# A streaming encoder step on one core: attention loads moved ahead, rope scores over 128 rows, another order of query tiles and fill

## The chip, the core and the metric

The kernel runs on one core of one Trainium2 chip. A core has five engines that run side by side, each with its own queue of instructions in a fixed order: TensorE (PE: matrix products, with weight loads as PEld), VectorE (DVE), ScalarE (ACT), GpSimd (POOL) and SyncE (SP, which here only issues transfers). They wait for each other by semaphores. The time is the device time of one execution in microseconds (us); the kernel before took 3075.96 us in the median of three runs (3072.53 to 3084.09).

## The reference

One inference step of a two-layer encoder over 1024 prompt rows and 32 sample rows (1056 together, width 1024). Layer 0 has a gated linear attention, layer 1 a latent attention (MLA) with 8 heads; each layer ends with a gated MLP (width 2816) with a causal convolution. The change touches the MLA:

```python
s = (jnp.einsum('bqhd,bkhd->bhqk', qn, k_nope) + jnp.einsum('bqhd,bkd->bhqk', qp, k_pe)) * scale
mask = k_chunk[None, :] <= (qpos // CHUNK)[:, None]          # CHUNK = 64
p = jax.nn.softmax(jnp.where(mask, s, -jnp.inf), axis=-1)
o = jnp.einsum('bhqk,bkhd->bqhd', p.astype(v.dtype), v)      # then o @ w_out, added to x
```

A query has a part of 128 numbers per head (`qn`, "nope") and a rotated part of 64 (`qp`, "rope"); `k_pe`, the rope key, is shared by the heads. Prompt queries see the prompt keys of their own 64-row chunk and of those before; sample queries see 512 cached keys and their own 32. All is float32.

## The kernel before

**Precision.** Most products are made of three passes in the fast float32 form (fp32r): each operand is split into a high part (a copy by ScalarE into fp32r) and a low part (raw minus high, by GpSimd). `mm3` (lines 275 to 277) then issues high x high, high x low, low x high. The splits of the attention are `akh`/`akl` (keys), `aqh`/`aql` (queries), `aph`/`apl` (rope queries), `kph`/`kpl` (rope keys), `moh`/`mol` (output weights) and `oh`/`ol` (attention output).

**Stages.** Layer 0, then the latent projection (`act_mla`, `dve_mla`, `pe_mla`: among others the rope keys, with cached ones in columns 1024 to 1535), then for four pairs of heads the projections of keys, values and queries (`PREP`, a list of units; results go to DRAM by `sp_prep`), then attention, then layer 1's MLP.

**Attention.** 72 steps, 9 per head: `STEPS` (line 1335) takes tiles t = 0 to 7 (128 queries against 128(t+1) keys) and then t = 8 (32 sample queries against 544 keys), ascending in each head. In step s TensorE does, in this order (`pe_att`): the scores of step s in pieces of up to 512 keys (`score`), the transposes of the probabilities of step s-1 (`turn`, line 1423, and 1425 for the 32 queries), a fill tile, the weighing of the values of step s-2 (`weigh`, line 1439), and another fill tile. Between scores and transposes the step goes through VectorE (mask 1561, maximum 1563, negation 1565), ScalarE (exponential 1518) and VectorE again (reciprocal 1569, scaling of `aP` 1571). ScalarE also copies the transposes out (1511) and makes `oh` (1528); VectorE makes `ol` (1578).

A piece of scores is an `mm3` over the 128 nope rows and an `mm3` over 64 rope rows. The rope queries of two heads lie in one buffer, in rows 0 to 63 and 64 to 127; the rope keys stand in both halves.

**Fill.** The output projection of a pair (24 tiles, each six matmuls of 352 columns into bank 7, then an addition on VectorE, line 443) is spread over the steps of the next pair by `FILL`: two tiles a step in steps 2 to 13 of 18. The last pair's 24 tiles come after all steps.

**Loads.** SyncE issues all transfers in one queue. `sp_att` loads keys (`load_k`), queries, rope queries (once a pair) and values of heads 0 and 1 behind everything that `sp_prep` stores, later heads two ahead of use. The output weights have one buffer: their load waits for the fill of the pair before, and the loads of heads 4 and 6 stand behind it. ScalarE's splits of head h+1 stand in its queue at tiles 3 (keys), 4 (queries) and, per pair, 6 (rope queries) of head h, the output weights at tile 7 of odd heads.

## Time and profile before

| | |
|---|---|
| median of 3 runs | 3075.96 us (3072.53 to 3084.09) |
| the profiled execution | 3070.57 us |
| its span, first to last instruction | 3068.6 us |
| mean granted TensorE clock | 0.959 |
| PE busy | 2852.2 us, 93% |
| PEld busy | 2680.6 us, 87% |
| DVE busy | 1202.8 us, 39% |
| ACT busy | 897.5 us, 29% |
| POOL busy | 690.2 us, 22% |
| chain that ended last | PE 39%, issue 36%, POOL 13%, DVE 8%, ACT 3%, DMA 1% |

A busy TensorE is not one at its peak: a matmul's record covers its way through the array, and records overlap. The distance from the start of one matmul to the start of the next is what it costs in a stream. "Clock" is the share of 2.4 GHz that was granted; 0.50 is 1.2 GHz. The chain is followed back from the last instruction through what released each one; "issue" is time in which nothing that the profile shows was waited for.

### The profile page before, as it was taken

Reading aid. Unit: us, or ns where it says so; the run is one execution under the profiler, and the core shown is the slowest. Engines: PE = TensorE matmul, PEld = TensorE weight load, DVE = VectorE, ACT = ScalarE, POOL = GpSimd, SP = SyncE. Lnnn points to the kernel's source line nnn. Section 1 sums busy time; section 2 is a strip of 40 time slices with the busy share of each in tenths; the row PEclk is TensorE's granted clock in tenths of the full one; section 3 lists DMA queues with packets and bytes.
Section 4 is the critical chain, followed back from the end, with each engine's and each line's share of the span. In section 5 each row is a group of like instructions: output and inputs, shape, how many; then the busy total and the mean of one; then the engine's idle time right before and its main releaser. Section 6 shows DMA issues by size and latency. Waiting matters only on the chain.

```text
span 3068.6 us, 42405 instructions
## 1 busy us (share of the span) xinstructions
PE 2852.2 (93%) x17373; PEld 2680.6 (87%) x17373; DVE 1202.8 (39%) x2169; ACT 897.5 (29%) x1530; POOL 690.2 (22%) x233
## 2 busy tenths in 40 slices
PE   6899999989999999999799969897989999999998
PEld 4888898979999999999788857676779999999998
DVE  5534443444333233324623334444463233233333
ACT  4332323243111111112346644233332211111111
POOL 2111111123322222231321112112032322322230
PEclk8899999999999999999999979898989999999999
DMA  2011111011111111111113231102001111111112
GB/s 93 16 32 30 31 43 31 30 31 42 42 43 47 51 42 42 56 42 42 60 53 119 106 140 64 49 29 77 28 14 56 42 42 55 43 42 42 56 42 72
DMA packets 155743, 154.74 MB, mean 50 GB/s; under 512 B 14897, under 2 KB 137407, under 8 KB 155439
## 3 DMA queue, kind: packets, MB, share of 16 engines
q1 hardware_dynamic: 153231, 150.03, 15.1%
q8 instruction: 150, 2.46, 0.3%
q10 hardware_dynamic: 2336, 2.03, 0.2%
q14 instruction: 26, 0.21, 0.0%
HBM read 125.89 MB, written 26.15 MB: 50 GB/s over the span
## 4 chain that ended last, share of the span: by engine, by line
PE 39%; issue 36%; POOL 13%; DVE 8%; ACT 3%; DMA 1%; SPq 0%; POOLq 0%; ACTq 0%; DVEq 0%
POOL wlo L256 9%; PE ps L275 9%; PE ps L276 8%; PE ps L277 8%; POOL falo L624 3%; PE ps L1439 2%; PE ps L1232 1%; PE ps L1423 1%; DVE ge L919 1%; PE ps L692 1%; DVE sq_rest L336 1%; DMA apraw<-s_p 1%; DVE xT L443 1%; PE ps L679 1%; DVE aP L1571 1%
## 5 line engine op out<-in xcount | busy, mean ns | idle before, releaser
L275 PE MATMUL ps<-hh,whi 128*128 128x352 f32 (+1 forms) x2688 | 879.9, 327 | 40.7 <-POOL hl L399 12.6
L276 PE MATMUL ps<-hl,whi 128*128 128x352 f32 (+1 forms) x2688 | 867.7, 323 | 0.0
L277 PE MATMUL ps<-hh,wlo 128*128 128x352 f32 (+1 forms) x2688 | 867.0, 323 | 0.0
L256 POOL TENSOR_TENSOR wlo<-wraw,whi 128x2048 fp32r<-128x2048 f32 (+1 forms) x87 | 393.8, 4527 | 970.3 <-ACT whi L249 923.0
L275 PEld LDWEIGHTS ps<-hh,whi 128*128 128x128 f32 (+1 forms) x2688 | 506.4, 188 | 51.7 <-issue 47.6
L276 PEld LDWEIGHTS ps<-hl,whi 128*128 128x128 f32 (+1 forms) x2688 | 507.4, 189 | 3.5 <-issue 1.1
L277 PEld LDWEIGHTS ps<-hh,wlo 128*128 128x128 f32 (+1 forms) x2688 | 505.8, 188 | 2.4 <-issue 0.2
L443 DVE TENSOR_TENSOR xT<-xT,ps 128x352 f32<-128x352 f32 x720 | 374.0, 521 | 340.2 <-PE ps L277 339.1
L275 PE MATMUL ps<-fahi,whi 128*128 128x352 f32 x1056 | 346.2, 328 | 16.2 <-POOL falo L624 10.4
L276 PE MATMUL ps<-falo,whi 128*128 128x352 f32 x1056 | 342.8, 325 | 0.0
L277 PE MATMUL ps<-fahi,wlo 128*128 128x352 f32 x1056 | 342.7, 325 | 0.0
L249 ACT ACTIVATE whi<-wraw 128x2048 fp32r<-128x2048 f32 (+1 forms) x83 | 157.2, 1894 | 632.4 <-DMA wraw<-w_ffn_in 453.9
L583 DVE TENSOR_SCALAR fc<-fg,par 128x1058 f32<-128x1058 f32 x44 | 39.1, 889 | 517.1 <-ACT fg L561 517.1
L624 POOL TENSOR_TENSOR falo<-fa,fahi 128x1056 fp32r<-128x1056 f32 x44 | 108.2, 2459 | 582.6 <-ACT fahi L566 582.6
L275 PEld LDWEIGHTS ps<-fahi,whi 128*128 128x128 f32 x1056 | 200.4, 190 | 23.7 <-DVE xT L443 12.2
L276 PEld LDWEIGHTS ps<-falo,whi 128*128 128x128 f32 x1056 | 200.3, 190 | 0.5 <-issue 0.5
L277 PEld LDWEIGHTS ps<-fahi,wlo 128*128 128x128 f32 x1056 | 200.2, 190 | 0.0
L599 DVE TENSOR_TENSOR fa<-fc,ps 128x352 f32<-128x352 f32 (+2 forms) x176 | 63.7, 425 | 249.3 <-PE ps L277 247.0
L566 ACT ACTIVATE fahi<-fa 128x1056 fp32r<-128x1056 f32 x44 | 47.8, 1086 | 265.1 <-DVE fa L599 265.1
L564 ACT ACTIVATE fc<-fc 128x1058 f32<-128x1058 f32 x44 | 48.0, 1090 | 184.7 <-DVE fc L593 184.7
L1511 ACT ACTIVATE aPT<-ps 128x384 f32<-128x384 f32 (+3 forms) x112 | 47.0, 449 | 179.1 <-PE ps L1423 154.8
L1439 PE MATMUL ps<-aPT,av 128*128 128x128 f32 (+2 forms) x656 | 95.4, 295 | 0.8 <-DVE ol L1578 0.8
(269 smaller groups left out, 4206.8 us busy)
## 6 DMA issues: line engine op xcount, KB each, us to landing
wraw<-w_ffn_in SPq DMA_DIRECT2D x88, 512.0 KB, 5.0
wraw<-w_ffn_out SPq DMA_DIRECT2D x44, 512.0 KB, 4.0
wraw<-w_gla_in SPq DMA_DIRECT2D x24, 512.0 KB, 4.6
s_k<-kw SPq DMA_DIRECT2D x8, 784.0 KB, 3.3
akraw<-s_k SPq DMA_DIRECT2D x8, 784.0 KB, 5.5
s_v<-vst SPq DMA_DIRECT2D x8, 768.0 KB, 3.9
av<-s_v SPq DMA_DIRECT2D x8, 768.0 KB, 5.8
s_q<-qw SPq DMA_DIRECT2D x8, 528.0 KB, 2.7
```

The source lines that it names most:

```text
L249: act.activation(hi[:, 0:cols], raw[:, 0:cols], ACT.Copy).then_inc(S("w_hi"), 1)
L256: pool.tensor_tensor(lo[:, 0:cols], raw[:, 0:cols], hi[:, 0:cols].bitcast(F32), ALU.subtract).then_inc(S("w_lo"), 1)
L275: nc.tensor.matmul(out, w[0], x[0], start=start, stop=False)
L276: nc.tensor.matmul(out, w[0], x[1], start=False, stop=False)
L277: return nc.tensor.matmul(out, w[1], x[0], start=False, stop=stop)
L443: dve.tensor_tensor(xT[:, m, tc(j)], xT[:, m, tc(j)], ps[:, banks[i % len(banks)], 0:TC], ALU.add)\
L564: act.activation(fc[:, par_, 0:CW], fc[:, par_, 0:CW], ACT.Gelu).then_inc(S("gelu"), 1)
L566: act.activation(fahi[:, gpar, par_, :], fa32[:, gpar, par_, :], ACT.Copy).then_inc(S("a_hi"), 1)
L599: last = dve.tensor_tensor(fa32[:, gpar, par_, t0:t0 + n], fc[:, par_, col:col + n], ps[:, B_BANKS[j], a:a + n], ALU.mult)
L624: pool.tensor_tensor(falo[:, gpar, par_, :], fa32[:, gpar, par_, :], fahi[:, gpar, par_, :].bitcast(F32), ALU.subtract).then_inc(S("a_lo"), 1)
L1439: last = pe.matmul(ps[:, 6, 0:m], av[h % 2][0:n, kk0 // P, :], aPT[s % 2][0:n, i, 0:m], start=(i == 0), stop=(i == len(tiles) - 1))
L1511: act.activation(buf[:, i0:i0 + nt, 0:m], src[:, :, 0:m], ACT.Copy).then_inc(S("probsT"), 1)
```

## The change

- **Rope scores.** `khl` takes the place of `kpl`: high rope keys in rows 0 to 63, low ones in rows 64 to 127. `kph` keeps the high keys in rows 0 to 63, and its rows 64 to 127 are made zero by subtracting them from themselves. The rope queries of a head are loaded twice, into both halves of a buffer of its own. One matmul of `aph` with `khl` then gives high x high + high x low, one of `apl` with `kph` low x high: two matmuls of 128 rows for three of 64. ScalarE and GpSimd split rope queries for each head instead of each pair. The latent projection has three ScalarE copies more into `khl` and one VectorE subtraction (64 x 1568) more.
- **Loads.** Head 0 is loaded in `sp_prep` of the last pair behind the value stores, head 1 behind its rope store; ScalarE's splits of head 0 stand behind the last query unit instead of behind all units. The output weights have two buffers: the load for pair p waits only for the fill of the pair two before.
- **Order.** Even heads take tiles 7, 6, 5, 4, 3, 8, 2, 1, 0, odd heads 0, 1, 2, 8, 3, 4, 5, 6, 7. The splits keep their place in the head (its steps 3, 4 and now 5; the output weights step 7 of the odd head).
- **Fill.** One tile in steps 2 to 4 and 14 to 16, two in steps 5 to 13.

```diff
-        K_AT, KL_AT = (W, H), (W + 4096, H + NKEY)
+        K_AT, KL_AT = (W + 2048 - NKEY, H), (W + 4096, H + NKEY)
...
-        moh = at("moh", [P, 2 * D], W + 2048, F32R)
...
+        MO_AT, MOL_AT = (R + 18272 - 176 - 2352, W + 2048), (W + 2048 - NKEY - 2 * D, R + 6 * NKEY)
+        moh = [at(f"moh{i}", [P, 2 * D], MO_AT[i], F32R) for i in range(2)]
...
+        def load_p(sp, h):
+            for a in range(2):
+                sp.dma_start(apraw[h % 2][a * ROPE:(a + 1) * ROPE, :],
+                             A["s_p"][h // 2][h % 2 * ROPE:(h % 2 + 1) * ROPE, :]).then_inc(S(f"head_loaded{h % 2}"), 16)
...
+            if p == MP - 1:
+                sp.wait_ge(S("k_left0"), 16)
+                load_k(sp, 0)
+                wait_unit(sp, (p, "v", 0, 6))
+                wait_unit(sp, (p, "k", 1, 3))
+                sp.wait_ge(S("q_left"), 16)
+                load_q(sp, 0)
+                sp.wait_ge(S("p_left"), 16)
+                load_p(sp, 0)
+                sp.wait_ge(S("v_left"), 64)
+                load_v(sp, 0)
             if p:
                 k_out(1)
             sp.wait_ge(S("rope_sum"), NCH * (p + 1))
             sp.dma_start(A["s_p"][p], pw[:, :]).then_inc(S("p_left"), 16)
+            if p == MP - 1:
+                wait_unit(sp, (p, "q", 1, 2))
+                sp.wait_ge(S("k_left1"), 16)
+                load_k(sp, 1)
+                load_q(sp, 1)
+                load_v(sp, 1)
+                sp.wait_ge(S("k_left0"), 16 * MP)
+                load_p(sp, 1)
             q_out(1)
...
-        STEPS = [(h, t) for h in range(MH) for t in range(9)]
+        UP = [0, 1, 2, 8, 3, 4, 5, 6, 7]
+        STEPS = [(h, t) for h in range(MH) for t in (UP if h % 2 else UP[::-1])]
...
-        FILL = [0, 0] + [2] * 12 + [0] * 4
+        FILL = [0, 0, 1, 1, 1, 2, 2, 2, 2, 2, 2, 2, 2, 2, 1, 1, 1, 0]
...
-                    last = mm3(out, (aph[pr][half, qs_], apl[pr][half, qs_]), (kph[half, keys], kpl[half, keys]),
-                               False, True)
+                    pe.matmul(out, aph[sl][:, qs_], khl[:, keys], start=False, stop=False)
+                    last = pe.matmul(out, apl[sl][:, qs_], kph[:, keys], start=False, stop=True)
...
-                    pe.wait_ge(S("o_lo"), NS - 9 + (3, 6, 9)[i // KD])
+                    pe.wait_ge(S("o_lo"), NS - 9 + (3, 7, 9)[i // KD])
...
-                if h % 2:
-                    sp.wait_ge(S("down_mm"), fill_before(h // 2))
-                    load_mo(h // 2)
+                if h % 2 == 0:
+                    sp.wait_ge(S("down_mm"), fill_before(h // 2 - 1))
+                    load_mo(sp, h // 2)
...
+            act.activation(khl[0:ROPE, 0:SEQ], kpe[0:ROPE, 0:SEQ], ACT.Copy)
...
+                if PREP[u] == (MP - 1, "q", 1, 2):
+                    head_split(act, 0)
+                    q_split(act, 0)
+                    p_split(act, 0)
...
+            dve.tensor_tensor(kph[low, :], kph[low, :].bitcast(F32), kph[low, :].bitcast(F32), ALU.subtract)\
+               .then_inc(S("latent_lo"), 1)
```

SyncE's queue at the end of the projections, before (`s_p`, `s_q`, `s_k`, `s_v` are the DRAM buffers, `kw`, `vst`, `pw` and `qw` what is stored there, the names in `raw` and `av` what attention reads):

```order
149 L1330 DMA s_p<-pw 128x1056
150 L1315 DMA s_q<-qw 128x1056
151 L1594 DMA akraw_142<-s_k 128x1568
152 L1597 DMA aqraw_148<-s_q 128x1056
153 L1600 DMA apraw_154<-s_p 128x1056
154 L1604 DMA av_156<-s_v 128x1536
155 L1606 DMA av_156<-s_v 32x128
156 L1594 DMA akraw_143<-s_k 128x1568
```

and now:

```order
148 L1298 DMA akraw_142<-s_k 128x1568
149 L1301 DMA aqraw_148<-s_q 128x1056
150 L1305 DMA apraw_154<-s_p 64x1056 x2
151 L1310 DMA av_156<-s_v 128x1536
152 L1312 DMA av_156<-s_v 32x128
153 L1335 DMA s_k<-kw_119 128x1568
154 L1365 DMA s_p<-pw 128x1056
155 L1298 DMA akraw_143<-s_k 128x1568
156 L1301 DMA aqraw_149<-s_q 128x1056
157 L1310 DMA av_157<-s_v 128x1536
158 L1312 DMA av_157<-s_v 32x128
159 L1305 DMA apraw_155<-s_p 64x1056 x2
```

The four loads of head 0 moved ahead of the last key and rope stores; those of head 1 stand between the rope store and the last query store, with the rope queries last.

TensorE's queue within head 0, the 640-key tile and the start of the next, before (`akh`, `akl`, `aqh`, `aql` nope keys and queries, `kph`, `kpl`, `aph`, `apl` rope ones, `aP` probabilities, `aPT` their transposes, `av` values):

```order
4432 L275 MATMUL ps<-akh_138,aqh_144 128x128
4433 L276 MATMUL ps<-akl_140,aqh_144 128x128
4434 L277 MATMUL ps<-akh_138,aql_146 128x128
4435 L275 MATMUL ps<-kph,aph_150 128x128
4436 L276 MATMUL ps<-kpl,aph_150 128x128
4437 L277 MATMUL ps<-kph,apl_152 128x128
4438 L1423 MATMUL ps<-ident,aP_159 128x128 x4
4439 L1439 MATMUL ps<-aPT_160,av_156 128x128 x3
4440 L275 MATMUL ps<-akh_138,aqh_144 128x512
```

and now, in its second step (the 896-key tile, behind the 1024-key one):

```order
4407 L276 MATMUL ps<-akh_138,aqh_144 128x512
4408 L277 MATMUL ps<-akl_140,aqh_144 128x512
4409 L278 MATMUL ps<-akh_138,aql_146 128x512
4410 L1450 MATMUL ps<-khl,aph_150 128x512
4411 L1451 MATMUL ps<-kph,apl_152 128x512
4412 L276 MATMUL ps<-akh_138,aqh_144 128x384
4413 L277 MATMUL ps<-akl_140,aqh_144 128x384
4414 L278 MATMUL ps<-akh_138,aql_146 128x384
4415 L1450 MATMUL ps<-khl,aph_150 128x384
4416 L1451 MATMUL ps<-kph,apl_152 128x384
4417 L1466 MATMUL ps<-ident,aP_158 128x128 x8
```

A piece of scores has five matmuls instead of six, all of them over 128 rows, and the eight transposes of the largest tile now come behind the second step's scores.

## Rows read from the trace of the kernel before

**Rows 1.** Stretches; columns in the first line.

```profile
core 0: us, PE busy (x) PEld busy (x) DVE busy (x) ACT busy (x) POOL busy (x), PEclk, DMA share, GB/s
1796.22:1819.81 23.59, 0.00 (x0) 0.03 (x1) 3.32 (x6) 5.09 (x5) 8.23 (x3) 0.60 0.77 296
1819.81:1889.99 70.18, 67.91 (x388) 50.48 (x389) 36.37 (x101) 35.77 (x84) 16.19 (x6) 0.92 0.13 44
1889.99:2005.73 115.74, 99.15 (x571) 81.11 (x570) 50.31 (x130) 38.12 (x91) 19.09 (x7) 0.88 0.14 52
...
2118.95:2229.45 110.50, 103.46 (x608) 85.25 (x606) 52.15 (x134) 35.91 (x93) 13.42 (x4) 0.93 0.11 36
1893.00:1900.00 7.00, 6.70 (x30) 6.35 (x31) 1.74 (x8) 1.13 (x6) 0.00 (x0) 0.51 0.00 1
1987.00:1995.00 8.00, 8.00 (x35) 6.29 (x36) 3.67 (x10) 2.61 (x7) 2.19 (x1) 0.69 0.00 0
```

**Rows 2.** Waits from 1796 to 2230: total, times, longest, in us.

```profile
ACT akh L1480 <- DMA apraw<-s_p: 46.0, 3, 17.6
...
PE ps L1423 <- DVE aP L1571: 27.8, 4, 13.4
...
PE ps L275 <- POOL apl L1588: 23.6, 1, 23.6
...
PE ps L1425 <- DVE aP L1571: 9.9, 4, 3.0
```

**Rows 3.** Timeline of TensorE, scores of a 1024-key tile: start, length.

```profile
1931.39 0.39 PE L275 MATMUL ps<-akh,aqh 128*128 128x512 f32 x1
1931.62 0.39 PE L276 MATMUL ps<-akl,aqh 128*128 128x512 f32 x1
...
1933.63 0.40 PE L277 MATMUL ps<-akh,aql 128*128 128x512 f32 x1
1933.96 0.50 PE L275 MATMUL ps<-kph,aph 64*128 64x512 f32 x1
1934.30 0.39 PE L276 MATMUL ps<-kpl,aph 64*128 64x512 f32 x1
1934.53 0.38 PE L277 MATMUL ps<-kph,apl 64*128 64x512 f32 x1
1934.85 0.98 PE L1423 MATMUL ps<-ident,aP 128*128 128x128 f32 x7
```

**Rows 4.** Timeline of SyncE: transfers issued.

```profile
1779.64 0.50 SPq L1325 DMA_DIRECT2D s_v<-vst  x1
...
1800.24 0.46 SPq L1594 DMA_DIRECT2D akraw<-s_k  x1
...
1971.82 0.43 SPq L1594 DMA_DIRECT2D akraw<-s_k  x1
```

**Rows 5.** GpSimd's subtractions by form: busy us, mean ns of one.

```profile
L1588 POOL TENSOR_TENSOR akl<-akraw,akh 128x1568 fp32r<-128x1568 f32 x8 | 28.2, 3522 | 289.5 <-ACT akh L1480 289.5
...
L1588 POOL TENSOR_TENSOR mol<-moraw,moh 128x2048 fp32r<-128x2048 f32 x4 | 18.0, 4512 | 79.0 <-ACT moh L1543 79.0
...
L1588 POOL TENSOR_TENSOR apl<-apraw,aph 128x1056 fp32r<-128x1056 f32 x4 | 9.8, 2442 | 23.1 <-ACT aph L1488 23.1
```

**Rows 6.** Timeline of VectorE: mask and scaling of one step, and a held scaling.

```profile
1849.26 0.11 DVE L1561 MEMSET ps<- 64x64 f32 x1 [1.61 <-PE ps L277]
...
1852.29 0.75 DVE L1571 TENSOR_SCALAR aP<-aP,rl 128x1024 f32<-128x1024 f32 x1
...
1890.24 3.00 DVE L1571 TENSOR_SCALAR aP<-aP,rl 32x544 f32<-32x544 f32 x1
```

**Rows 7.** Timeline in the latent projection: ScalarE's copy, and TensorE's wait.

```profile
1532.71 0.60 ACT L1789 ACTIVATE kph<-ps 128x512 fp32r<-128x512 f32 x1
...
1535.76 0.63 PE L275 MATMUL ps<-hh,whi 128*128 128x352 f32 x1 [3.18 <-ACT cqr L1794]
```

More of the change, by code:

```diff
@@ L1294, in dve_unit, with load_k, load_q, load_v @@
                                          ALU.mult, ALU.mult).then_inc(S("normed"), 1)
+        def load_k(sp, h):
+            sp.dma_start(akraw[h % 2][:, :], A["s_k"][h]).then_inc(S(f"head_loaded{h % 2}"), 16)
+        def load_q(sp, h):
+            sp.dma_start(aqraw[h % 2][:, :], A["s_q"][h]).then_inc(S(f"head_loaded{h % 2}"), 16)
+        def load_p(sp, h):
+            for a in range(2):
+                sp.dma_start(apraw[h % 2][a * ROPE:(a + 1) * ROPE, :],
+                             A["s_p"][h // 2][h % 2 * ROPE:(h % 2 + 1) * ROPE, :]).then_inc(S(f"head_loaded{h % 2}"), 16)
+        def load_v(sp, h):
+            n = (KT - 1) * P
+            sp.dma_start(av[h % 2][:, 0:KT - 1, :].rearrange("p t v -> p (t v)"), A["s_v"][h][:, 0:n])\
+              .then_inc(S(f"av_loaded{h % 2}"), 16)
+            sp.dma_start(av[h % 2][0:DEC, KT - 1, :], A["s_v"][h][0:DEC, n:n + P])\
+              .then_inc(S(f"av_loaded{h % 2}"), 16)
+        def load_mo(sp, p):
+            v = moraw[p % 2][:, :].rearrange("p (k n) -> p k n", k=2)
+            for a in range(2):
+                sp.dma_start(v[:, a, :], w_mout[:, 2 * p + a, :]).then_inc(S("mo_loaded"), 16)
         def sp_prep(sp, p):
@@ L1365, in fill_before, with mo_view @@
             return 24 * (B_MLA + p)
-        def mo_view():
-            return [w[:, :].rearrange("p (k n) -> p k n", k=2) for w in (moh, mol)]
+        def mo_view(p):
+            return [w[p % 2][:, :].rearrange("p (k n) -> p k n", k=2) for w in (moh, mol)]
         def pe_pair_tile(pe, p, i, bank):
@@ L1374, in pe_pair_tile @@
             for k in range(2):
-                last = mm3(ps[:, bank, 0:TC], [v[:, k, m * P:(m + 1) * P] for v in mo_view()],
+                last = mm3(ps[:, bank, 0:TC], [v[:, k, m * P:(m + 1) * P] for v in mo_view(p)],
                            (oh[o][:, k, tc(j)], ol[o][:, k, tc(j)]), k == 0, k == 1)
@@ L1380, in build @@
         LAST_BANKS = (7, 4, 5, 6)
-        SPLITS = [("k", 0), ("q", 0), ("p", 0), ("k", 1), ("q", 1)]
-        for h in range(2, MH):
-            SPLITS += [("k", h), ("q", h)] + ([("p", h // 2), ("mo", h // 2 - 1)] if h % 2 == 0 else [])
+        SPLITS = []
+        for h in range(MH):
+            SPLITS += [("k", h), ("q", h), ("p", h)] + ([("mo", h // 2 - 1)] if h and h % 2 == 0 else [])
         SPLITS += [("mo", MP - 1)]
@@ L1525, in act_att @@
                     act.wait_ge(S("att_mm"), s - 1)
-                    if t == 0 and h % 2 == 0 and p >= 2:
+                    if (s - 2) % 18 == 0 and p >= 2:
                         act.wait_ge(S("down_mm"), fill_before(p - 1))
@@ L1561, in dve_att @@
                         dve.memset(flat[0:64, c0 + nk - 64:c0 + nk], MASKED).then_inc(S("masked"), 1)
-                        dve.wait_ge(S("masked"), h * 8 + t + 1)
+                        dve.wait_ge(S("masked"), sum(t_ < NG for _, t_ in STEPS[:s + 1]))
                     dve.tensor_reduce(mx[0:m, two], flat[0:m, c0:c0 + nk], AX.X, ALU.max).then_inc(S("max"), 1)
@@ L1788, in act_mla @@
             act.wait_ge(S("cache_mm"), 3)
[L1789 removed]
+            act.activation(kph[:, SEQ:SEQ + PAST], ps[:, A_BANKS[0], 0:PAST], ACT.Copy)
+            act.activation(khl[0:ROPE, SEQ:SEQ + PAST], ps[0:ROPE, A_BANKS[0], 0:PAST], ACT.Copy)\
+               .then_inc(S("latent_hi"), 1)
             act.wait_ge(S("kpe_sb"), 1)
```

120 lines of the change are left out of this document (43 added, 77 removed).

## Prediction

> **What bounds the kernel now.** I read the page first: TensorE is busy 93% of the span, and the chain that ended last is a third TensorE work, a third "issue". So the place to look is where TensorE is not doing useful columns. The change touches only the attention stage and a few instructions of the latent projection ahead of it, so I cut that stage out with stretches of time [rows 1]: attention with its fill runs from 1819.81 to 2229.45, 409.6 us, as one pair of heads without fill (70.2 us) and three pairs with 24 fill tiles each (115.7, 113.2 and 110.5; the middle one is what the other stretches leave of the 409.6). Before it TensorE stands still for 23.6 us, at a mean clock of 0.60.
>
> The waits of that stage [rows 2] name three kinds of idle time: 23.6 us once, for the low half of the rope queries (GpSimd); 27.8 us in four waits, the longest 13.4, for the softmax's scaled rows; 9.9 us in four waits for the same thing ahead of the 32-row tile. ScalarE's 46.0 us for a DMA say why the first two exist: the key load of heads 4 and 6 leaves late [rows 4] and the cast of it stands in ScalarE's queue ahead of the exponentials.
>
> Then the matmuls one by one [rows 3]: with 128 rows behind 128 rows a 512-column matmul follows in 0.23 us (1931.39 to 1931.62). Between the nope part (128 rows) and the rope part (64 rows) it takes 0.33 (1933.63 to 1933.96) and the one after it 0.34; leaving the rope part takes 0.32 again (1934.53 to 1934.85). So each change of row count costs 0.21 us more than the columns do, and a 64-row matmul costs what a 128-row one does.
>
> **The change, part by part, against the profiled execution (3070.6 us; the runs' median is 3076.0, 5.4 above it).**
>
> *Rope scores in 128 rows.* (a) One of six matmuls of each score piece goes, 112 in all. Per head the pieces are seven of 512 columns, two of 384, two of 256, two of 128 and one of 32. At 0.23 for 512 and, in proportion with a floor near 0.12 (estimate; the weight load), 0.17, 0.12, 0.12, 0.03 for the others: 1.6 + 0.34 + 0.24 + 0.24 + 0.03 = 2.5 us a head. (b) The changes of row count go: 14 times into the rope part and 5 times out of it to a second piece, 0.21 each, and 9 times out of it to the transposes, of which I take only the half seen on the rope side (0.32 instead of 0.23 at 1934.53 to 1934.85), less 0.5 for the 32-row tile: 2.9 + 1.05 + 0.9 - 0.5 = 4.4 us a head. Together 6.9 us, times 8 = **-55 us** of TensorE work (bounds: 20, only the matmuls; 62, both halves of each change).
>
> The Trainium skill ("TensorEngine Tiling (Array Packing)", Key Properties) says that a change of tiling mode drains the engine. The rows above agree for 128 to 64 rows. By the rule read strictly the 32-query tile is a change too and would keep its cost, some 0.2 us twice a head, 3 us in all; the sum above is without it.
>
> *Loads in order.* The loads of head 0 stood behind the last query store, at 1800.24. Now they follow the value stores of the last pair, which left by 1779.64 + 0.50 [rows 4]; about 2.7 MB at 385 GB/s (296 at a DMA share of 0.77 in the gap, [rows 1]) is there by 1790. ScalarE casts them behind the last query copy (about 1793.5 by my estimate, some 2.7 us before TensorE ends the projection at 1796.2), GpSimd's three subtractions follow from 1795.0: 3.5 + 2.5 + 2.4 [rows 5] = 8.4, so scores start at 1803.5. The gap shrinks from 23.6 to 7.3: **-16.3**. What is late next is GpSimd, no longer a DMA. Nothing hides that chain.
>
> With two buffers for the output weights, the loads of heads 4 and 6 no longer wait for the fill of the pair before. The two stalls (13.4 and 12.3, in the 27.8 of [rows 2]) go, and with each the slow clock behind it: 8 us at 0.69 [rows 1] are 2.5 us each. **-30**. Head 4's loads leave at step 27 and its cast stands at step 30, some 13 us later, for a 7 us transfer: covered.
>
> *What the same edits add.* Head 1's loads now stand behind rope_sum, which DVE finishes only behind GpSimd's subtractions (its SBUF-to-SBUF operations hold while GpSimd runs: a scaling of 544 columns took 3.00 us at 1890.24 beside the 4.5 us subtraction, where one of 1024 takes 0.75 [rows 5, 6]), near 1804.5. Four loads, 3.2 MB with the store ahead, land near 1814; the cast of head 1's keys stands in ScalarE's queue behind the first exponential, about 1811: 3 us of waiting, with the exponentials of step 1 behind it and TensorE behind these.
>
> *Order of the tiles.* In head 0, the large tile comes first: its chain (mask, maximum, exponential, scaling) is 1849.26 to 1853.04, 3.8 us [rows 6], and 4.1 with the hops, and only 2.4 us of score matmuls stand beside it. VectorE is at both ends of that chain, so no step is shorter than its chain. With TensorE's work cut (a 1024-key step: ten score matmuls 2.4, and by estimate from the tiles' number transposes 0.8 and weighing 1.25, together 4.5 instead of 5.6) the steps of small tiles without fill become chain-bound: 128 to 512 keys have a chain of about 1.9 to 2.7 (estimate from the same chain with fewer columns) against 0.9 to 1.8 of TensorE work. In pair 0 that is 5 us over six steps, 3 at the start, 3 for the load above, about 4 for the half clock under large tiles instead of small ones, 2 for GpSimd's subtractions under shorter steps: **+17**. Pair 0 keeps its 70 us or so, its 14 us of saved TensorE work gone.
>
> In pairs 1 to 3 every step has TensorE work above its chain (smallest margin: the 1024-key steps, 4.4 against 4.1), because the fill is spread over steps 2 to 16: the fill of 24 tiles itself stays the same. The first of these pairs shows 99.2 us of busy TensorE in 115.7 [rows 1]; the clock's deficit is 0.12 of 115.7 = 13.9 us, about 8 of it inside the 16.6 us in which TensorE stood, so some 5.6 us of the busy time are slow clock and 93.6 are work. Less 2 x 6.9 that is 80 us a pair.
>
> *GpSimd.* Four rope subtractions more (2.4 each). Their casts stand where steps take 4 to 5 us with fill, and VectorE's scaling falls outside. The output weight's subtraction (4.5 us) now stands one step earlier, under the scaling of the last 1024-key tile: 2.0 us late instead of the 2.5 before the 32-row tile, with 2.4 us of scores beside it instead of 0.85. Before it cost 2.3 us and 7 us at half clock, 3.4 lost [rows 1]. I take 2 us less over the four, and 2 less for waits behind the first fill tile: **-2 to -4**, taken as -2.
>
> The Trainium skill ("SBUF — State Buffer", Who interferes with whom) says that the shared port is an exclusive lock for a tensor_scalar in a fast mode and for a tensor_tensor with both inputs in SBUF, and that the later one blocks to the end. The 3.00 us row agrees. By the rule at its worst, all 85 us of GpSimd's passes lie over a VectorE scaling, each up to its own length; that is rival 2 below.
>
> *Projection.* ScalarE has 0.6 us more (the copy of the cached rope keys, [rows 7]) ahead of the logarithm for which TensorE waits 3.2 us: **+0.5**. The other copies and VectorE's subtraction of the rows with themselves stand beside matmuls of 11 us and cost nothing; without that cover they would cost 3.
>
> Sum: -55 - 16.3 - 30 - 2 + 17 + 0.5 = **-86**, and 2 us less at the end, where the large tile's wait of about 4 us is followed by half of the transposes and weighings that stood there: -88. Profile 2983, median 2988.
>
> **The rivals.**
> 1. *Only the matmuls go* (10%). What I read as the cost of changing the row count comes from new weights and stays. For: the extra is at both ends of a group. Against: fill to nope has none of it. Then -88 + 35 = -53: 3023.
> 2. *Short steps run into the chain, the loads and GpSimd's lock* (15%). Pair 0 costs 85 instead of 71, and each of pairs 1 to 3 loses 4 us more under the casts, with the clock falling behind each gap, as it did for 7 us behind one of 2.3. -88 + 26: 3014. For: the margins of the 1024-key steps are 0.3 us. Against: the three pairs with fill had only the waits named in [rows 2].
> 3. *Slower: the clock* (3%). TensorE now has idle time in nearly every step of pair 0 and less work in the others, and the granted clock stays at its lower level (1.2 GHz) instead of 2.4 through much of the stage. The stage has some 315 us of work: from 90 us of work at half clock on, the gain is used up; with half the stage, 157 us, it is slower by 70: 3146. For: it was 0.51 in the 7 us behind a short wait [rows 1]. Against: pair 0 of before, short steps and a cold start in it, still had 0.92 on the mean [rows 1].
> 4. *More than I take* (7%): both halves of every change of row count go (7 us more) and the first steps hide the load: 2972.
>
> **How the numbers follow.** 65% for the forecast, 2972 to 3003 its own range. Rivals 1 and 2 reach to 3023, so the range is 2966 to 3023. A measurement of this kernel tells 0.5% (15 us) from no change. Faster by more than that: all but rival 3, and what I can't name: 0.94; within 0.02; slower 0.04.
>
> **What would show it.** In the profile after: score matmuls of 512 columns following each other in 0.23 with no 0.33 among them; TensorE's gap ahead of attention near 7 us, ended by GpSimd; no wait over 5 us at heads 4 and 6; pair 0 near 70 us and pairs 1 to 3 near 82 to 85 each. I am wrong if pair 0 grows beyond 80, if the pairs with fill stay above 92, or if a step with fill waits for VectorE.

## The result, and the profile after

The changed kernel took 2972.40 us in the median of four runs (2969.68 to 2973.62), the kernel before 3074.99 in four runs beside it (3072.53 to 3084.09): a ratio of 0.966, 95% interval 0.9639 to 0.9681. The forecast was 2988 with a range of 2966 to 3023. The direction and the range held; the gain is 15 us larger than forecast (102.6 for 88).

The profiled execution after took 2972.77 us, its span is 2970.7 at a mean clock of 0.969. First the same stretches as in [rows 1]: the gap ahead of attention, then the four pairs of heads, the last up to the first tile of its own output projection (columns: stretch, us, busy us of each engine with its instructions, granted clock, DMA share, GB/s).

```profile
1803.43:1811.16 7.73, 0.00 (x1) 0.03 (x1) 7.52 (x4) 3.06 (x5) 7.59 (x3) 0.78 0.00 0
1811.16:1879.55 68.39, 56.28 (x359) 48.94 (x359) 37.14 (x104) 35.49 (x85) 18.58 (x7) 0.90 0.38 128
1879.55:1961.83 82.28, 79.46 (x544) 72.70 (x542) 49.45 (x130) 39.23 (x92) 22.22 (x8) 1.00 0.25 79
1961.83:2043.44 81.61, 79.49 (x543) 72.66 (x542) 48.77 (x130) 39.21 (x92) 21.56 (x8) 1.00 0.24 80
2043.44:2135.12 91.68, 85.83 (x582) 78.69 (x580) 51.32 (x134) 38.50 (x94) 15.71 (x5) 0.98 0.13 40
```

Attention is 323.96 us long where it was 409.64 (-85.7), and the gap ahead of it 7.73 where it was 23.59 (-15.9); the two make 101.5. (The two profiled executions differ by 97.8: in the one after, the projections ended 7.2 us later, and what lies behind attention was 3.6 shorter.) Of the 85.7, pair 0 gives 1.8, the next two pairs 33.5 and 31.6, the last 18.8. The two pairs that lost most are those in which a stall of 13.4 and 12.3 us stood. The clock is at 1.00 through both now; it was 0.88 and 0.91.

What TensorE waited for in attention after (view of the waits: total, times, longest), in answer to [rows 2]:

```profile
PE ps L1466 <- DVE aP L1611: 18.3, 14, 7.1
PE ps L276 <- POOL apl L1628: 7.7, 1, 7.7
PE ps L276 <- DVE xT L444: 3.4, 12, 0.4
...
PE ps L1468 <- DVE aP L1611: 0.4, 1, 0.4
```

The wait for scaled rows has gone from 27.8 us in four to 18.3 in fourteen: the two long stalls went, and one of 7.1 us and thirteen of 0.3 to 2.9 came. The 9.9 us ahead of the 32-row tile are 0.4.

Scores of a 1024-key tile after, on TensorE's timeline, in answer to [rows 3]:

```profile
1958.42 0.39 PE L1451 MATMUL ps<-kph,apl 128*128 128x512 f32 x1
1958.64 0.40 PE L276 MATMUL ps<-akh,aqh 128*128 128x512 f32 x1
1958.88 0.40 PE L277 MATMUL ps<-akl,aqh 128*128 128x512 f32 x1
1959.12 0.40 PE L278 MATMUL ps<-akh,aql 128*128 128x512 f32 x1
1959.35 0.39 PE L1450 MATMUL ps<-khl,aph 128*128 128x512 f32 x1
1959.58 0.39 PE L1451 MATMUL ps<-kph,apl 128*128 128x512 f32 x1
1959.81 0.38 PE L1466 MATMUL ps<-ident,aP 128*128 128x128 f32 x2
```

Every start is 0.22 to 0.24 behind the one before, into and out of the rope part too; the 0.33 are gone.

The new wait of 7.1 us is the one thing in this profile that the forecast had much smaller. Its story, on four engines (start, length; in brackets the idle time ahead and what ended it):

```profile
1800.62 1.51 ACT L1521 ACTIVATE akh<-akraw 128x1568 fp32r<-128x1568 f32 x1
1800.95 0.52 DVE L1285 TENSOR_TENSOR pw<-pw,cos 128x352 f32<-128x352 f32 x1
1802.21 3.51 POOL L1628 TENSOR_TENSOR akl<-akraw,akh 128x1568 fp32r<-128x1568 f32 x1 [47.65 <-ACT akh L1521]
1802.64 3.46 DVE L1285 TENSOR_TENSOR pw<-pw,cos 128x352 f32<-128x352 f32 x1
1811.50 0.53 DVE L1288 TENSOR_TENSOR pw<-pw,arp 128x352 f32<-128x352 f32 x1
1812.06 0.32 SPq L1365 DMA_DIRECT2D s_p<-pw  x1
1823.63 1.51 ACT L1521 ACTIVATE akh<-akraw 128x1568 fp32r<-128x1568 f32 x1 [5.36 <-DMA apraw<-s_p]
1829.25 1.76 PE L1466 MATMUL ps<-ident,aP 128*128 128x128 f32 x7 [7.11 <-DVE aP L1611]
```

GpSimd starts on head 0; the rotation of the rope queries on VectorE, whose multiplications take 0.52 us, takes 3.46 beside it; SyncE, which waits for the last sum, issues the rope store at 1812.06 and head 1's loads behind it; ScalarE waits 5.36 us for them with an exponential behind, and TensorE 7.11.

### The profile page after: what moved, and what is told of

It reads as the page before. It is cut to its first block, busy times and chain, and to the rows that moved or that the text cites. A ratio compares the mean times of both kernels' runs of the same rounds, so it can differ in the third digit from the quotient of the medians.

```text
span 2970.7 us, 42205 instructions
## 1 busy us (share of the span) xinstructions
PE 2787.6 (94%) x17261; PEld 2659.4 (90%) x17261; DVE 1210.4 (41%) x2170; ACT 903.0 (30%) x1537; POOL 702.0 (24%) x237
## 4 chain that ended last, share of the span: by engine, by line
PE 38%; issue 37%; POOL 13%; DVE 8%; ACT 2%; DMA 0%; SPq 0%; POOLq 0%; ACTq 0%; DVEq 0%
POOL wlo L257 10%; PE ps L276 8%; PE ps L277 7%; PE ps L278 7%; POOL falo L625 3%; PE ps L1482 2%; PE ps L1233 1%; PE ps L693 1%; DVE ge L920 1%; PE ps L1466 1%; DVE xT L444 1%; DVE sq_rest L337 1%; PE ps L680 1%; DVE h L353 1%; DVE aP L1611 1%
## 5 line engine op out<-in xcount | busy, mean ns | idle before, releaser
L276 PEld LDWEIGHTS ps<-fahi,whi 128*128 128x128 f32 x1056 | 200.6, 190 | 23.7 <-DVE xT L444 12.2
L276 PE MATMUL ps<-gahi,whi 128*128 128x352 f32 x192 | 69.6, 363 | 21.7 <-DVE xT L444 11.0
L1482 PE MATMUL ps<-aPT,av 128*128 128x128 f32 (+2 forms) x656 | 88.4, 281 | 0.8 <-DVE ol L1618 0.8
```

What stands on the lines that cost most here:

```text
L276: nc.tensor.matmul(out, w[0], x[0], start=start, stop=False)
L1482: last = pe.matmul(ps[:, 6, 0:m], av[h % 2][0:n, kk0 // P, :], aPT[s % 2][0:n, i, 0:m], start=(i == 0), stop=(i == len(tiles) - 1))
```

## Experiments

Each is the kernel after with the one edit shown. "Attention" is measured as above. The projections end between 1794.5 and 1807.7 us in the profiles of all fourteen kernels, and at 1803.4 and 1797.2 in two of the same kernel, so a single profile's total says little to 7 us, while the gap repeats to 0.01 and attention to 2.6 us (the wait for head 1's load was 7.1 in one and 9.5 in the other). Ratios are to runs of the kernel before that were taken beside it, with their 95% intervals.

| kernel | median us | ratio | gap | pair 0 | 1 | 2 | 3 | attention |
|---|---|---|---|---|---|---|---|---|
| before | 3074.99 | 1 | 23.6 | 70.2 | 115.7 | 113.2 | 110.5 | 409.6 |
| after | 2972.40 | 0.9660 (0.9639 to 0.9681) | 7.7 | 68.4 | 82.3 | 81.6 | 91.7 | 324.0 |
| after, again | 2970.42 | 0.9659 (0.9635 to 0.9683) | 7.7 | 71.2 | 82.3 | 81.6 | 91.3 | 326.5 |
| rope in 64 rows | 3008.47 | 0.9786 (0.9761 to 0.9812) | 7.7 | 79.0 | 93.5 | 93.4 | 100.6 | 366.5 |
| rope 3 x 128 rows | 2981.12 | 0.9698 (0.9676 to 0.9721) | 7.7 | 74.9 | 85.6 | 84.8 | 92.8 | 338.1 |
| first steps in 64 rows | 2970.63 | 0.9659 (0.9639 to 0.9679) | 7.7 | 67.0 | 82.3 | 81.6 | 90.0 | 321.0 |
| old fill | 2971.82 | 0.9663 (0.9639 to 0.9687) | 7.7 | 70.8 | 81.9 | 81.8 | 92.4 | 326.8 |
| old fill and wait | 3012.73 | 0.9788 (0.9761 to 0.9814) | 7.7 | 70.6 | 102.4 | 102.2 | 92.3 | 367.5 |
| late loads | 2979.61 | 0.9686 (0.9665 to 0.9708) | 26.2 | 60.0 | 82.3 | 81.6 | 90.1 | 314.0 |
| head 1 early | 2959.55 | 0.9622 (0.9602 to 0.9642) | 7.7 | 60.2 | 82.3 | 81.6 | 90.1 | 314.2 |
| casts sooner | 2961.37 | 0.9648 (0.9630 to 0.9665) | 6.0 | 60.4 | 82.2 | 81.6 | 90.0 | 314.3 |
| tiles ascending | 2987.18 | 0.9724 (0.9706 to 0.9741) | 7.7 | 73.5 | 83.4 | 84.9 | 95.3 | 337.2 |
| weights in halves | 2965.47 | 0.9654 (0.9638 to 0.9670) | 7.7 | 66.7 | 80.8 | 80.8 | 88.0 | 316.3 |
| early and halves | 2955.83 | 0.9621 (0.9599 to 0.9644) | 7.7 | 60.1 | 80.8 | 80.8 | 88.0 | 309.7 |

The kernel after, again:

> The kernel after, unchanged, as the reference for the others of this call, and to see how much of the difference outside attention belongs to the execution: in the profile of after the projections ended at 1803.4 us, in that of before at 1796.2, in two kernels derived from after at 1796.5 and 1797.5. Theory 'it is the execution': this profile ends them anywhere from 1794 to 1805, and attention takes 324 us again within 1. Rival 'it belongs to the kernel': 1803 to 1804 again.

The projections ended at 1797.2: the 7 us by which the first profile of after was late outside attention belong to the execution. Attention did not repeat within 1 us: it took 326.5, with 2.4 us more of waiting for head 1's load.

**What the rope form is worth.** Two kernels. Rope scores in 64 rows again:

```diff
-                    pe.matmul(out, aph[sl][:, qs_], khl[:, keys], start=False, stop=False)
-                    last = pe.matmul(out, apl[sl][:, qs_], kph[:, keys], start=False, stop=True)
+                    half = slice(ROPE, P)
+                    last = mm3(out, (aph[sl][half, qs_], apl[sl][half, qs_]), (kph[half, keys], khl[half, keys]), False, True)
...
-            dve.tensor_tensor(kph[low, :], kph[low, :].bitcast(F32), kph[low, :].bitcast(F32), ALU.subtract)\
-               .then_inc(S("latent_lo"), 1)
```

(`kph` keeps the high keys in rows 64 to 127 here, since the subtraction that made them zero is gone.)

> The kernel after, with one thing back: the rope scores of a piece are three matmuls of 64 rows (high x high, high x low, low x high, read from rows 64 to 127 of the same buffers) in place of two of 128 rows. Same output. My theory (one matmul costs its columns, 2.5 us a head; each change between 128 and 64 rows costs 0.21 us more, 4.4 us a head): about +50 us against after (42 to 58, somewhat under 55 where a step of pair 0 is held by its softmax chain), and the trace shows starts 0.33 apart at the way into the rope part and behind its first matmul again. Rival 'only the matmul count': +20 (15 to 25), starts 0.23 apart throughout. Rival 'the gain of the stage is the loads and the order, not the rope': under +10.

And three matmuls of 128 rows:

```diff
+                    pe.matmul(out, apl[sl][:, qs_], kph[:, keys], start=False, stop=False)
                     last = pe.matmul(out, apl[sl][:, qs_], kph[:, keys], start=False, stop=True)
```

> The kernel after with the second rope matmul of each piece (low queries x high keys, 128 rows) issued twice: three matmuls of 128 rows, so the count of before without its changes of row count. The low part of the rope queries is counted twice in the scores. My theory: only the count is back, +20 us against after (14 to 24), so some 30 us below the 64-row form. Rival 'only the matmul count matters, the row count costs nothing': within 5 us of the 64-row form. Rival 'the row change is all': within 5 us of after.

Measured: 64 rows +40.0 to +42.6 us of attention (by the ratios 0.9786 - 0.9660, 39 us), at the foot of the 42 to 58 expected or under it; 3 x 128 rows +11.6 to +14.2, under or at the foot of 14 to 24. Yet the TensorE work is what the forecast said. The 64-row form, one 1024-key tile:

```profile
1971.60 0.39 PE L278 MATMUL ps<-akh,aql 128*128 128x512 f32 x1
1971.92 0.49 PE L276 MATMUL ps<-kph,aph 64*128 64x512 f32 x1
1972.26 0.39 PE L277 MATMUL ps<-khl,aph 64*128 64x512 f32 x1
1972.49 0.39 PE L278 MATMUL ps<-kph,apl 64*128 64x512 f32 x1
1972.81 0.50 PE L276 MATMUL ps<-akh,aqh 128*128 128x512 f32 x1
1973.14 0.40 PE L277 MATMUL ps<-akl,aqh 128*128 128x512 f32 x1
```

and the 3 x 128-row form:

```profile
1958.76 0.39 PE L1450 MATMUL ps<-khl,aph 128*128 128x512 f32 x1
1958.99 0.39 PE L1451 MATMUL ps<-kph,apl 128*128 128x512 f32 x1
1959.22 0.39 PE L1452 MATMUL ps<-kph,apl 128*128 128x512 f32 x1
1959.45 0.39 PE L276 MATMUL ps<-akh,aqh 128*128 128x512 f32 x1
```

Scores of a 1024-key tile take 2.40 us after, 2.84 with the third 128-row matmul, 3.53 in 64 rows. Added up over the nine tiles of a head, where nothing waits: 12.6, 15.1 and 19.2. So a matmul more per piece is 2.5 us a head and the changes of row count 4.1, with the transposes behind them (0.93 against 0.87 us for eight) 4.3: the two terms of the forecast (2.5 and 4.4). 6.8 x 8 = 54 us of work against 40 to 43 of time: the difference is idle time. TensorE stood 7.3 us in the 366.5 of the 64-row form (366.51 - 359.19 busy) and 22.9 in the 324.0 of after. Work taken from TensorE came back as 15.6 us of waiting, 5.9 of it where head 1's load is waited for (7.1 us, 1.2 in the 64-row form). (54 less 15.6 is 38; the 4 more that the profile shows were not separated. The 64-row form spent 24 us at half clock behind the start, see below.)

**What the stalls at heads 4 and 6 were.** Old fill, and old fill with the loads of the output weights as before:

```diff
-        FILL = [0, 0, 1, 1, 1, 2, 2, 2, 2, 2, 2, 2, 2, 2, 1, 1, 1, 0]
+        FILL = [0, 0] + [2] * 12 + [0] * 4
...
-                if h % 2 == 0:
-                    sp.wait_ge(S("down_mm"), fill_before(h // 2 - 1))
+                if h % 2:
+                    sp.wait_ge(S("down_mm"), fill_before(h // 2))
```

The first hunk alone:

> The kernel after with the fill as before: two tiles in each of steps 2 to 13 of a pair, none in 14 to 16, where after has one in 2 to 4 and 14 to 16. My theory: with fill the steps have TensorE work above their chain; the last steps (1024-key tiles of the odd head at 15 to 17) have 4.4 to 4.8 us of own work against a chain of 4.1, the weights' subtraction stands there: +2 to +8 us over the three pairs. Rival 'the spread is what removes the chain-bound steps': +12 or more. Rival 'the fill's place is without effect': within 2 us.

Both hunks:

> The kernel after with the loads of the output weights as before: the load for pair p (p of 1 to 3) waits until the fill of pair p-1 has ended, and stands behind head 2p+1's loads, ahead of those of head 2p+2; and with the fill as before (two tiles in each of steps 2 to 13), because with the fill spread to step 16 this wait would never end. To be read against the kernel with the old fill alone. My theory: heads 4 and 6 are loaded late again, two stalls of 10 to 14 us each with slow clock behind: +26 us against old_fill (20 to 32), and the waits of TensorE for the scaled rows grow by 20 us or more at steps 31 and 49 of 72. Rival 'the stalls were of the ascending order or of the chip's contention, not of this wait': within 5 us of old_fill.

The fill alone changes nothing (attention 326.8 against 324.0 and 326.5, the medians within 1 us): I had expected 2 to 8, and the rival was right. With the wait TensorE stalls 16.96 and 16.65 us, ScalarE waits 45.6 us for the DMA in three waits, and the pairs with the two stalls take 102.4 and 102.2 in place of 81.9 and 81.8. So a stall of 17 costs 20.5; the 3.5 more goes with slow clock behind it (0.90 in these pairs, 1.00 without). The wait makes the stall: +40.8, where I expected 20 to 32. The stalls were longer than in before (13.4 and 12.3), probably because shorter steps leave the load less time; that was not tested.

**What the early loads are worth.** Late loads (both heads' loads behind everything, and ScalarE's casts of head 0 behind all its copies):

```diff
-            if p == MP - 1:
-                sp.wait_ge(S("k_left0"), 16)
-                load_k(sp, 0)
...
-                if PREP[u] == (MP - 1, "q", 1, 2):
-                    head_split(act, 0)
...
+            head_split(act, 0)
+            q_split(act, 0)
+            p_split(act, 0)
```

> The kernel after with the loads of heads 0 and 1 behind all stores of the projections again, and ScalarE's splits of head 0 behind all its copies. My theory (the gap ahead of attention is set by when head 0's loads leave): the gap grows from 7.7 to 22 to 25 us, and since head 1's loads follow at once, its wait stays: +15 us (12 to 19). Rival 'GpSimd's three subtractions are the gap, the loads are hidden': under +5. Rival 'head 1 is worse too': +20 or more.

And head 1 early:

```diff
-            sp.wait_ge(S("rope_sum"), NCH * (p + 1))
-            sp.dma_start(A["s_p"][p], pw[:, :]).then_inc(S("p_left"), 16)
             if p == MP - 1:
...
                 load_p(sp, 1)
+            sp.wait_ge(S("rope_sum"), NCH * (p + 1))
+            sp.dma_start(A["s_p"][p], pw[:, :]).then_inc(S("p_left"), 16)
```

> The kernel after with the four loads of head 1 issued ahead of the wait for the rope sums and of the store of the rope queries. In after ScalarE waits 5.4 us for the keys of head 1 and TensorE 7.1 us behind that, in pair 0. Theory 'the loads leave late because they stand behind the rope sum': both waits go (TensorE waits under 2.5 us there, for the chain), with slow clock behind it: pair 0 is 6 to 9 us shorter, 60 to 62, the median 6 to 9 us lower. Rival 'the wait is the chain of the 1024-key and 896-key tiles, the load lies beside it': under 2 us. Rival 'the earlier loads take the DMA engines from those of head 0': the gap ahead of attention grows from 7.7 by 2 us or more, and the median gains under 5.

With late loads the gap is 26.2, 18.5 more, above the 22 to 25 expected. But pair 0 falls to 60.0, since the loads of head 1 leave right behind those of head 0, inside the gap. The net is 5.9 to 8.5 us, 8 by the ratios, not the 12 to 19 expected: about half of what the early loads of head 0 bring (8.4 to 11.2 of 18.5) is lost again to the late ones of head 1. Head 1's loads ahead of the rope sum take that loss away: the gap stays at 7.74, and the pair that was 68.4 and 71.2 takes 60.2. Pair 0 of late loads, and of head 1 early, beside the second stretch of after above:

```profile
1826.26:1886.29 60.03, 53.35 (x359) 46.15 (x359) 34.65 (x101) 35.42 (x85) 18.61 (x7) 0.97 0.22 76
```

```profile
1815.42:1875.62 60.20, 53.53 (x358) 46.27 (x359) 36.64 (x104) 35.40 (x85) 18.58 (x7) 0.97 0.30 101
```

The wait of 7.1 us is 1.70 there. The median is 10.9 us under the unchanged kernel's beside it, a little more than the 6 to 9 expected; the intervals of the two ratios just overlap (up to 0.9642, from 0.9635).

Casts sooner is head 1 early, with ScalarE's casts of head 0 ahead of its last three query copies:

```diff
             for u in range(4, len(PREP)):
+                if PREP[u] == (MP - 1, "q", 1, 0):
+                    head_split(act, 0)
+                    q_split(act, 0)
+                    p_split(act, 0)
                 act_unit(act, u)
```

> The kernel with the loads of head 1 ahead of the rope sum, and in addition ScalarE's three casts of head 0 ahead of its last three query copies in place of behind them. In after ScalarE stood free from 1797.0 to 1798.4 and cast head 0 from 1800.6 on; GpSimd's three subtractions (8.9 us) are the whole gap. Theory 'the gap is GpSimd's start': it starts 3 us sooner, the gap shrinks from 7.7 to 4 to 5, the clock dips less, and the median is 3 to 5 us under that of the kernel with head 1's loads early (2959.6). Rival 'the query copies are late instead': TensorE's last squares and rotations wait for them up to 3.6 us, the projection ends later by as much as the gap shrinks, and the median is within 2 us. Rival 'head 0's loads have not landed at 1797': ScalarE waits for the DMA there, and the median is 1 to 4 us higher.

The theory failed: the gap is 6.03 and not 4 to 5, released by VectorE's rotation, and a new wait of 1.65 us for the squares of those copies stands ahead of it. 1.70 won, 1.65 lost, attention is the same (314.3 for 314.2), and the median 1.8 us higher, the ratio 0.0026 with intervals that overlap. That is the second rival's outcome, but the sign of the third is there too: ScalarE waited 2.01 us for head 0's load before its first cast.

**The order of the tiles.**

```diff
-        UP = [0, 1, 2, 8, 3, 4, 5, 6, 7]
-        STEPS = [(h, t) for h in range(MH) for t in (UP if h % 2 else UP[::-1])]
+        STEPS = [(h, t) for h in range(MH) for t in range(9)]
...
-                    pe.wait_ge(S("o_lo"), NS - 9 + (3, 7, 9)[i // KD])
+                    pe.wait_ge(S("o_lo"), NS - 9 + (3, 6, 9)[i // KD])
```

> The kernel after with the query tiles ascending in every head, as before (0 to 7, then the 32-row tile); rope form, loads and fill as in after. Theory from the traces of before and after: the order pays, because before had a wait of 2.3 us ahead of the 32-row tile at each end of a pair, with 7 us at half clock behind it, and because small tiles without fill at the start of a pair (0.5 us of scores each) leave their softmax chain of 1.6 to 1.9 us bare: +3 to +5 us in each of pairs 1 to 3, and in pair 0 the wait for the keys of head 1 grows by 1 to 3 us since less work lies beside it: +12 us (8 to 18). Rival 'the new order is what costs pair 0 its gain', as the forecast had it with a large tile at the start under half clock: pair 0 shorter by 5 us or more, the whole -5 to 0. Rival 'the order is without effect': within 3.

Attention is 10.7 to 13.2 us longer, the time by the medians 15 and by the ratios 20 (0.9724 against 0.9660, intervals 0.9706 to 0.9741 and 0.9639 to 0.9681). Three us more lie behind attention (839.4 to the end of the span, as in before 839.2, where after has 835.6); the other kernels spread there from 835.8 to 838.1, so the cause stays open. The waits of TensorE in its attention:

```profile
PE ps L1465 <- DVE aP L1610: 18.0, 9, 12.2
PE ps L1467 <- DVE aP L1610: 11.4, 4, 3.2
```

The second row is the wait ahead of the 32-row tile, 2.7 us or more at each end of a pair; after has 0.4 there. And the wait for head 1's load is 12.2, not 7.1, since two small tiles hide less of it than two large ones. The order pays, 8.2 us of it in pairs 1 to 3. In pair 0 it is 2.3 to 5.1, which is little beside the 2.8 by which the two profiles of after differ there.

**Weights in halves.**

```diff
-        SPLITS += [("mo", MP - 1)]
+        SPLITS += [("ma", MP - 1), ("mo", MP - 1)]
...
-                        act.activation(moh[p % 2][:, :], moraw[p % 2][:, :], ACT.Copy).then_inc(S("att_hi"), 1)
+                        act.activation(moh[p % 2][:, 0:D], moraw[p % 2][:, 0:D], ACT.Copy).then_inc(S("att_hi"), 1)
+                    if s % 9 == 8 and h % 2:
+                        act.activation(moh[h // 2 % 2][:, D:2 * D], moraw[h // 2 % 2][:, D:2 * D], ACT.Copy).then_inc(S("att_hi"), 1)
...
```

> The kernel after with the split of the output weights (128 x 2048) in two halves: ScalarE's copy and GpSimd's subtraction of the first half at step 7 of an odd head, of the second at step 8. In after the 4.5 us subtraction holds VectorE's scaling of the last 1024-key tile of a pair, and TensorE waits for it at the start of the next: 1.32, 0.63 and 0.63 us, 2.91 at the end. Theory 'the one long subtraction makes these waits': 1 to 3 us less over the whole. Rival 'the wait is the chain of two 1024-key tiles behind each other': the same waits within 0.2, the median within 2 us. Rival 'two passes lock twice': +1 to +4.

After, GpSimd and VectorE at the turn to pair 1:

```profile
1878.23 4.57 POOL L1628 TENSOR_TENSOR mol<-moraw,moh 128x2048 fp32r<-128x2048 f32 x1 [6.09 <-ACT moh L1583]
1880.80 2.55 DVE L1611 TENSOR_SCALAR aP<-aP,rl 128x1024 f32<-128x1024 f32 x1
1883.41 1.09 PE L1466 MATMUL ps<-ident,aP 128*128 128x128 f32 x8 [1.32 <-DVE aP L1611]
```

In halves:

```profile
1875.49 2.36 POOL L1631 TENSOR_TENSOR mol<-moraw,moh 128x1024 fp32r<-128x1024 f32 x1 [5.23 <-ACT moh L1583]
1878.92 0.75 DVE L1613 TENSOR_SCALAR aP<-aP,rl 128x1024 f32<-128x1024 f32 x1
```

The scaling that took 2.55 us beside the long subtraction takes 0.75 between two short ones, and the wait behind it is gone; pairs 1 to 3 are 1.5, 0.8 and 3.3 to 3.6 us shorter, and the wait at the end is 1.81 for 2.91. Not all of the 3.3 to 3.6 is the edit's: in both profiles of after the clock fell behind that wait (0.98 on the mean of the last pair), in those of late loads and head 1 early it did not behind the same wait (1.00), and there the last pair took 90.1, 2.0 us more than in halves. So the edit is worth 4.3 us, where 1 to 3 was expected. The median moves by 0.0006 of the ratio, which its interval does not tell from nothing.

**Early and halves**, the best of what the experiments point to:

> The kernel after with both: head 1's loads ahead of the rope sum, and the output weights' split in two halves. Attention took 324.0 and 326.5 us in two profiles of after, 314.2 with the early loads alone and 316.3 with the halves alone, in which pairs 1 to 3 took 80.8, 80.8 and 88.0 (88.0 without a slow clock before them) in place of 82.3, 81.6 and 90.1. Theory 'the two waits are independent': pair 0 60 us, attention 308 to 311, some 14 to 17 us under after, the ratio to before 0.961 (0.9595 to 0.9625). Rival 'the gain of the halves was the execution's': attention 313 to 315 again.

Attention 309.7, where 308 to 311 was expected: the two gains add. The ratio, 0.9621 in five runs, is under that of after by 0.0039, 12 us, with intervals that touch (0.9599 to 0.9644, 0.9639 to 0.9681); over head 1 early alone its advantage of 4.4 us is seen in the profile only.

**The clock behind the gap.** In the 64-row form the clock behind the start of attention stayed low much longer than after, behind the same gap. So the 64-row form in the first three steps alone (all three matmuls read rows 64 to 127, where `khl` holds the low keys, so the rope part of these tiles leaves out the high keys):

```diff
+                    if s < 3:
+                        dn = slice(ROPE, P)
+                        last = mm3(out, (aph[sl][dn, qs_], apl[sl][dn, qs_]), (khl[dn, keys], khl[dn, keys]), False, True)
+                    else:
...
```

> The kernel after with the rope scores of the first three steps of attention alone as three matmuls of 64 rows (all from rows 64 to 127, so the rope part of those three tiles is not the right one); the other 69 steps as in after. With the 64-row form everywhere the granted clock was 0.50 for 24 us behind the start of attention, in after it was 1.00 again within 4 us, behind the same gap of 7.7 us. Theory 'the 64-row matmuls keep the clock down': 0.50 for the first 12 us or more, pair 0 is 3 to 7 us longer than the 68.4 of after, pairs 1 to 3 the same. Rival 'the clock's return is a matter of the execution': 1.00 within 5 us of the start, and pair 0 at most 2 us longer.

From the start of attention, the kernel after:

```profile
1811.16:1815.16 4.00, 4.00 (x11) 3.17 (x12) 2.00 (x3) 0.00 (x0) 0.00 (x0) 0.57 0.60 184
1815.16:1819.16 4.00, 2.17 (x11) 1.64 (x9) 2.31 (x5) 1.20 (x2) 0.00 (x0) 1.00 1.00 392
```

and with the first three steps in 64 rows:

```profile
1805.62:1813.62 8.00, 8.00 (x16) 4.26 (x16) 3.48 (x6) 0.00 (x0) 0.00 (x0) 0.50 0.80 289
1813.62:1821.62 8.00, 8.00 (x22) 5.53 (x23) 2.27 (x5) 4.51 (x7) 1.72 (x1) 0.50 0.91 313
1821.62:1825.62 4.00, 4.00 (x15) 2.90 (x15) 3.27 (x5) 1.41 (x4) 4.00 (x2) 0.50 0.00 0
1825.62:1829.62 4.00, 4.00 (x30) 3.78 (x29) 1.10 (x4) 2.96 (x6) 0.94 (x2) 0.93 0.02 6
```

With 128-row matmuls the clock is back at 2.4 GHz within 4 us, with 64-row ones among them TensorE is busy without a pause for 20 us at 1.2 GHz. The first half of the theory held. The second did not: pair 0 is not longer (67.0), because the slow steps lie where after waits for head 1's load. Half clock in the place of a wait cost nothing here.

The form is not all that decides. Behind its wait of 7.1 us, which ends at 1829.25, after runs 128-row matmuls alone, and they stay at half clock for almost 6 us:

```profile
1827.16:1831.16 4.00, 1.91 (x9) 1.91 (x10) 3.22 (x5) 1.62 (x3) 4.00 (x2) 0.50 0.00 0
1831.16:1835.16 4.00, 4.00 (x19) 3.81 (x18) 1.08 (x3) 1.96 (x5) 0.32 (x1) 0.51 0.01 2
```

With the tiles ascending, 128-row matmuls of small tiles with pauses between them stayed at 0.50 through the first 8 us. In both kernels with 64-row matmuls the clock rose amid transposes and weighings, which have 128 rows. And the 64-row form everywhere, once up, stayed at 1.00 through pairs 1 and 2. What sets the return beyond this one comparison is open.

## Why the prediction was right, and where it was not

**Rope (-55).** Right as work, to the single terms: 2.5 and 4.3 us a head measured for 2.5 and 4.4, 54 us in all. Rival 1 (only the matmuls) is refuted: count alone brings 12 to 14 us of attention, the row changes 28. As time the form is worth 40 to 43. For the rest I had a term apart, pair 0's +17. By the rule of the Trainium skill ("TensorEngine Tiling (Array Packing)", Key Properties) that a change of tiling mode drains the engine, read strictly, the 32-row tile keeps its change. The trace agrees on the way in: in after, where all other starts are 0.23 apart, the way into its transposes keeps 0.1. On the way out it depends on what follows: into a fill tile 0.27 us, where it is 0.25 behind transposes of 128 rows too, into a weighing 0.21 for 0.11.

```profile
1939.51 0.39 PE L1450 MATMUL ps<-khl,aph 128*128 128x512 f32 x1
1939.74 0.40 PE L1451 MATMUL ps<-kph,apl 128*128 128x512 f32 x1
1940.07 1.25 PE L1468 MATMUL ps<-ident,aP 32*128 32x32 f32 x10
```

**Gap (-16.3).** -15.9, ended by GpSimd as forecast; the moments came as forecast too (cast of head 0, GpSimd's start and rope sum each within 0.5 us, counted from the end of the projections). But the edit is worth less than its term: against late loads it brings 18.5 in the gap and gives 8.4 to 11.2 back in pair 0.

**Pair 0 (+17, stays near 70).** 68.4 and 71.2, which is 11.8 and 14.6 more than 70.2 less the 13.6 of rope work. So the total was 2 to 5 us too high, and that it came so near is in part luck, for the parts came out otherwise and their errors cancel. The wait for head 1, 3 in the forecast, is worth 8.2 and 11.0 with the half clock behind it, as head 1 early shows: the loads left when I said, but ScalarE had them 20.2 us behind the end of the projections and not 17.8, so it waited 5.4 us (7.8 in the second profile) and TensorE 7.1 (9.5). The other step failed the other way: chain-bound small steps 5, start 3, half clock under large tiles 4 and GpSimd's lock 2 were to be 14, and come to 3.6 together (60.2 - 56.6). How the 3.6 divide, no run shows, but the half clock has the wrong sign: before spent its first 12 us of pair 0 at 0.51, head 1 early its first 4 at 0.56 and the rest at 1.00. Without the load's wait the pair is 10 us shorter than before.

**Stalls (-30).** Gone, both. Taking the last pair, which had none before, as base, pairs 1 and 2 gained 14.7 and 12.8 us more than it: 27.5.

**Order and GpSimd (-2, and -2 at the end).** The term of the sum that was most mis-sized, and the largest single reason why the gain came out larger. The order brings 11 to 13 us of attention, 8 of them in pairs 1 to 3 (83.4, 84.9 and 95.3 against 82.3, 81.6 and 91.5). I had seen the 2.3 us waits ahead of the 32-row tile with 3.4 us lost at each, and netted them against a subtraction that would hold the 1024-key scaling for 2.0 us. It holds it for 1.8 (2.55 for 0.75) and costs TensorE 1.3, 0.6 and 0.6 us at the turns of the pairs, and the clock stayed at 1.00 behind these. About 7 us more in pairs 1 to 3 than rope, stalls and order explain (83.9 - 40.8 - 27.5 - 8.2) I have not separated.

**Projection (+0.5).** TensorE's wait for the normalised latent is 3.63 us for 3.18. Right.

**Fill.** I gave it no term of its own; old fill shows none.

**The signs I named.** Pair 0 is under 80, the gap 7.7, starts 0.23 apart, no wait over 5 us at heads 4 and 6: as said. The last pair is 91.7 and not 82 to 85; I had not counted that its stretch holds the last two steps' tail and 3.7 us of waits. And steps with fill do wait for VectorE, 0.4 us once a pair for scaled rows and twice for the addition of a fill tile (once before): too little for rival 2, whose price for pair 0 (85) is refuted. Rival 3 is refuted too: the clock rose in every pair with fill. Rival 4 gave 2972, which is what was measured, but that is luck: the changes of row count gained no more than I took, and the first steps do not hide the load.

The Trainium skill ("SBUF — State Buffer", Who interferes with whom) calls VectorE's and GpSimd's shared port a lock held for a whole instruction. The trace agrees at two places that decide something here: the rotation's multiplication at 3.46 us for 0.52 beside a subtraction of 3.51, and the scaling at 2.55 for 0.75. Three operations of the rotation take 3.46, 2.54 and 2.10 us for some 0.53 each, 6.5 us more in all; the rope sum ended 8.6 us behind the projections, in before, where no subtraction ran beside it, 2.4. So the lock makes the rope sum late, and with it head 1's loads. No run took the lock away; head 1 early took the loads from behind it.

## What to carry to other kernels

When a load moves forward, look at what stands in front of the next load in the same queue: here half the gain of head 0's loads went into head 1's, which stood behind a sum that the earlier work itself had slowed. Matrix products that alternate between 128 and 64 rows pay at each change, and here kept the clock low for longer behind a gap; filled up with zero rows the same number of products took 28 us of attention less. And before work is taken off the busiest engine, count the steps that are already near their chain: more than a quarter of the work saved here (15.6 us of 54) came back as waiting, more than a third of that for one late load.
